# A transformer kernel with streamed weights: low parts written over the raw steps, experts written out, the first norm moved into the first modulation

## The reference, cut to what matters

```python
def first_block(x, c, w_ada, ...):                    # two layers
    cs = jax.nn.silu(c)
    for l in range(DEPTH):
        mod = cs @ w_ada[l] + b_ada[l]
        shift, scale, gate = mod[:, None, :D], mod[:, None, D:2 * D], mod[:, None, 2 * D:]
        h = rmsnorm(x, g_pre[l]) * (1.0 + scale) + shift
        y = hybrid_mixer(h, ...)                      # block attention, compressed and windowed attention
        x = x + gate * rmsnorm(y, g_post[l])
    return x
def second_block(x, c, w_ada, ...):
    # layer 0: neighbourhood attention, then a gated feed-forward of width 2816
    # layer 1: latent attention, then 8 experts of width 1792, the best 2 per token
    ...
        x = x + g_a[:, None, :] * m
        h = _modulate(x, sh_f, sc_f)
        ...
        x = x + g_f[:, None, :] * f
    return _rmsnorm(x) * final_norm
```

## Time and profile before

| what | us |
|---|---|
| median of 3 runs (lowest, highest) | 1647.71 (1645.18, 1649.2) |
| profiled execution | 1648.49 |
| its span | 1646.7 |
| mean granted clock of PE | 0.94 |
| PE busy | 1420.0 |
| DVE busy | 1216.3 |
| ACT busy | 861.3 |
| POOL busy | 65.5 |

### The profile page before, as it was taken

One profiled execution on the slowest core, in us unless ns is written; L12 is line 12 of the kernel. 1 busy time (PEld: TensorE's weight loads), 2 busy tenths in 40 slices (PEclk: granted clock), 3 DMA queues, 4 the chain that ended last, 5 costly groups with the idle time before them and its releaser, 6 DMA issues.

```text
span 1646.7 us, 21231 instructions
## 1 busy us (share of the span) xinstructions
PE 1420.0 (86%) x7628; PEld 1189.7 (72%) x7628; DVE 1216.3 (74%) x1484; ACT 861.3 (52%) x1210; POOL 65.5 (4%) x82
## 2 busy tenths in 40 slices
PE   2798996989869986899985896999999999999992
PEld 1687776877658865898974785877777777777772
DVE  8676657766566646788866535889889888899885
ACT  0443544435443543344323544577677777777772
POOL 0000000000010000000001004000000000000001
PEclk9989998999988997999997996999999999999996
DMA  9763524735246632677773214799999999999782
GB/s 400 296 258 110 198 103 162 283 118 193 102 155 254 238 120 97 258 309 282 267 270 122 103 52 145 272 342 364 353 343 366 341 351 366 336 368 353 289 366 89
DMA packets 61538, 403.08 MB, mean 245 GB/s; under 512 B 6535, under 2 KB 9735, under 8 KB 15117
## 3 DMA queue, kind: packets, MB, share of 16 engines
q1 hardware_dynamic: 52416, 379.45, 60.7%
q10 hardware_dynamic: 7020, 15.17, 2.6%
q0 software_dynamic: 2016, 7.34, 1.2%
HBM read 393.01 MB, written 8.91 MB: 244 GB/s over the span
## 4 chain that ended last, share of the span: by engine, by line
PE 49%; DVE 31%; ACT 9%; issue 7%; DMA 2%; POOL 1%; ACTq 0%; DVEq 0%; SPq 0%; POOLq 0%
DVE w_lo L2175 18%; PE PS L826 13%; PE PS L828 12%; PE PS L827 12%; ACT w_hi L1601 4%; DVE acc L2192 3%; ACT xg L1695 2%; PE PS L978 1%; PE PS L998 1%; DMA raw<-in_ws 1%; DVE a_lo L2335 1%; PE PS L896 1%; DVE hb L2346 1%; DVE hb L2344 1%; DVE h_lo L2301 1%
## 5 line engine op out<-in xcount | busy, mean ns | idle before, releaser
L2175 DVE TENSOR_TENSOR w_lo<-raw,w_hi 128x2048 fp32r<-128x2048 f32 x287 | 659.5, 2298 | 147.7 <-ACT w_hi L1601 124.8
L1601 ACT ACTIVATE w_hi<-raw 128x2048 fp32r<-128x2048 f32 x287 | 547.7, 1918 | 235.1 <-PE PS L828 222.9
L826 PE MATMUL PS<-w_hi,h_hi 128*128 128x512 f32 (+2 forms) x812 | 336.6, 415 | 24.7 <-DVE h_lo L2596 7.3
L827 PE MATMUL PS<-w_lo,h_hi 128*128 128x512 f32 (+2 forms) x812 | 319.4, 393 | 0.0
L828 PE MATMUL PS<-w_hi,h_lo 128*128 128x512 f32 (+2 forms) x812 | 319.2, 393 | 0.0
L826 PE MATMUL PS<-h_hi,w_hi 128*128 128x256 f32 x776 | 235.4, 303 | 24.1 <-DVE h_lo L2220 11.2
L828 PE MATMUL PS<-h_hi,w_lo 128*128 128x256 f32 x776 | 227.1, 293 | 0.0
L827 PE MATMUL PS<-h_lo,w_hi 128*128 128x256 f32 x776 | 227.1, 293 | 0.0
L826 PEld LDWEIGHTS PS<-w_hi,h_hi 128*128 128x128 f32 x812 | 156.3, 192 | 72.0 <-DVE w_lo L2175 15.1
L2192 DVE SCALAR_TENSOR_TENSOR acc<-raw,cs,acc 128x512 f32<-128x512 f32 x252 | 189.5, 752 | 8.9
L828 PEld LDWEIGHTS PS<-w_hi,h_lo 128*128 128x128 f32 x812 | 156.1, 192 | 32.7
(11 more groups left out here) (310 smaller groups left out, 1405.8 us busy)
## 6 DMA issues: line engine op xcount, KB each, us to landing
raw<-in_ws SPq DMA_DIRECT2D x359, 1024.0 KB, 5.7
y_rows<-ysb ACTq DMA_DIRECT2D x10, 512.0 KB, 7.0
rp<-in_rp ACTq DMA_DIRECT2D x8, 384.0 KB, 4.7
ckb<-in_ck ACTq DMA_DIRECT2D x2, 1024.0 KB, 4.8
y_rows<-ones ACTq DMA_DIRECT2D x3, 512.0 KB, 9.2
x<-in_x SPq DMA_DIRECT2D x1, 1024.0 KB, 11.3
gpost<-in_gpost ACTq DMA_DIRECT2D x2, 512.0 KB, 5.3
x_rows<-xn_f ACTq DMA_DIRECT2D x2, 512.0 KB, 3.8
```

The lines of the kernel that those rows point to most:

```text
L826: t.matmul(out, lhs[0], rhs[0], start=start, stop=False, skip_group_check=True)
L827: t.matmul(out, lhs[0], rhs[1], start=False, stop=False, skip_group_check=True)
L1601: a.activation(wh[:, SPL_AT[e.phase][i], :], raw[:, r, :], ACT.Copy).then_inc(*e.inc("hi"))
L2175: v.tensor_tensor(wl[:, s, :], raw[:, r, :], wh[:, s, :].bitcast(F32), ALU.subtract).then_inc(*e.inc("raw_used"))
```

## The change

1. The rings: RAW is 8 instead of 6, SPL 4 instead of 3, and w_lo has no ring of its own: it is written over the raw step it is made of (twelve places of 8 KB per partition as before). A weight step's raw place is therefore released by PE's `split_used`, a half's as before by `raw_used`. `hi_to` and `split_to` go one step further in most places.
2. The experts are written out, moe0 to moe7, on every engine; only `more` is a loop.
3. pre holds units 0 to 3 (8 halves). x is fetched behind its fourth step, lc behind its eighth. ACT's squares and DVE's xn of the first norm stand inside pre, PE's turn behind unit 1. ACT makes the w_hi of four steps before the scaled half of h; DVE makes w_lo(0) behind h_lo. The gate units 4 and 5 of the first layer are summed behind w2 to w5 of lay0 and added on PE between its first slots; the gate's product with gpost stands in tick 1.
4. Halves stand elsewhere: in the layers behind w7 to w15 (nothing behind w2 to w5 in lay1), in na as formerly in the layers (none behind w6). PE adds units 0 and 1 in ticks 1 and 4 instead of before tick 0.

```diff
-RAW = 6
-SPL = 3
+RAW = 8
+SPL = 4
-LAY_ADA = {9: 2, 10: 3, 12: 4, 15: 5}
+LAY_ADA = {1: 0, 4: 1, 9: 2, 10: 3, 12: 4, 15: 5}
...
-def layer_steps():
-    halves = dict(zip((2, 3, 4, 5, 7, 8, 9, 10, 11, 12, 13, 14), (x for j in range(6) for x in ada_steps(j))))
+def layer_steps(gates):
+
+    place = [(6, 0, 0), (7, 0, 1), (8, 1, 0), (8, 1, 1), (9, 2, 0), (10, 2, 1), (10, 3, 0), (11, 3, 1),
+             (12, 4, 0), (13, 4, 1), (13, 5, 0), (14, 5, 1)]
     out = []
     for n in range(20):
         out.append(("w", n))
-        if n in halves:
-            out.append(halves[n])
+        if gates and n in (2, 3, 4, 5):
+            out.append(("ada", 4 + (n - 2) // 2, n % 2))
+        out += [("ada", j + 6 * gates, half) for after, j, half in place if after == n - 1]
     return out
...
-    halves = dict(zip(range(2, 14), (x for j in range(6) for x in ada_steps(j))))
+    halves = dict(zip((2, 3, 4, 5, 7, 8, 9, 10, 11, 12, 13, 14), (x for j in range(6) for x in ada_steps(j))))
...
+def raw_released(p, i):
+
+    if STEPS[p][i][0] == "w":
+        return "split_used", STEPS[p][i][1]
+    return "raw_used", i
+
+
+RAW_AT, RAW_NEED = ring_plan(RAW, {p: len(STEPS[p]) for p in PHASES}, raw_released)
+SPL_AT, SPL_NEED = ring_plan(SPL, SPLITS, lambda p, i: ("split_used", i))
...
-        wl = sb("w_lo", [P, SPL, STEP], F32R)
+
+        wl = nc.alloc_sbuf_tensor_at("w_lo", [P, RAW, STEP], F32R, offset=at[0] - 4 * RAW * STEP - 4 * SPL * STEP)
...
-                        sp.wait_ge(*e.at("raw_used", RAW_NEED[phase][i]))
+                        sp.wait_ge(*e.at(*RAW_NEED[phase][i]))
...
+                    if phase == "pre" and i == 3:
+                        sp.dma_start(x[:], dram["x"]).then_inc(*e.inc("x_in", 16))
+                    if phase == "pre" and i == len(STEPS[phase]) - 1:
+                        sp.dma_start(lc[:], dram["lc"]).then_inc(*e.inc("lc_in", 16))
...
+                    if i in (2, 5):
+                        pe.wait_ge(*e.at("bank3", used[3]))
...
+                    if i == 1:
+                        pe.wait_ge(*e.at("cmp_u", 1))
+                    if i == 4:
+                        pe.wait_ge(*e.at("clogits", 1))
                     if i in LAY_ADA:
-                        ada(LAY_ADA[i])
+                        ada(unit + LAY_ADA[i])
...
-                with dve.Fori(0, LOOPS) as rep:
-                    for p in TWO:
-                        start(p, rep)
-                        expert()
-                start("moeZ")
-                expert()
+                for p in EXPERTS[1:]:
+                    start(p)
+                    expert()
...
-                        v.tensor_tensor(wl[:, s, :], raw[:, r, :], wh[:, s, :].bitcast(F32),
+                        v.tensor_tensor(wl[:, r, :], raw[:, r, :], wh[:, s, :].bitcast(F32),
                                         ALU.subtract).then_inc(*e.inc("raw_used"))
...
+            raw_to(4)
+            e.enter("lay0")
+            normed(xn_l)
+            e.resume("pre")
             raw_to(99)
...
-                    split_to(min(na_steps_before(i) + SPL, 15) if i < 14 else 16)
+                    split_to(min(na_steps_before(i) + SPL, 16))
```

More of the change, by code:

```diff
@@ L31 @@
 T_CMP = 15
-PHASES = ["pre", "lay0", "lay1", "na", "ffn", "mla", "rt", "go", "moe0", "moeA", "moeB", "moeZ", "more", "end"]
+EXPERTS = [f"moe{i}" for i in range(NEXP)]
+PHASES = ["pre", "lay0", "lay1", "na", "ffn", "mla", "rt", "go"] + EXPERTS + ["more", "end"]
 MORE = 2 * S // (P + 1)
 ROUNDS = NEXP + MORE
-TWO = ("moeA", "moeB")
-LOOPS = (NEXP - 2) // 2
-REPS = {"moeA": LOOPS, "moeB": LOOPS, "more": MORE}
-EXPERTS = [("moe0", 0)] + [(p, r) for r in range(LOOPS) for p in TWO] + [("moeZ", 0)]
-KIND = {"lay0": "lay", "lay1": "lay"}
+REPS = {"more": MORE}
+KIND = {"lay0": "lay", "lay1": "lay", **{p: "moe" for p in EXPERTS}}
 LAY_FEAT = (0, 1, 4, 5)
@@ L129 @@
 STEPS = {
-    "pre": [x for j in range(6) for x in ada_steps(j)],
-    "lay0": layer_steps(),
-    "lay1": layer_steps(),
+    "pre": [x for j in range(4) for x in ada_steps(j)],
+    "lay0": layer_steps(True),
+    "lay1": layer_steps(False),
     "na": na_steps(),
@@ new lines, in ring_plan @@
+        for _ in range(reps):
+            here = dict(totals)
+            for i in range(n):
+                last = owner[place[p][i]]
+                if last is not None:
+                    k = (last[0], last[1] + 1 - here.get(last[0], 0))
+                    assert need[p][i] is None or need[p][i][0] == k[0]
+                    need[p][i] = k if need[p][i] is None else max(need[p][i], k)
+                name, j = released(p, i)
+                owner[place[p][i]] = (name, here.get(name, 0) + j)
+            for name, n_ in (("raw_used", len(STEPS[p])), ("split_used", SPLITS[p])):
+                totals[name] = totals.get(name, 0) + n_
@@ L204 @@
+    "act_lo": {"moe": 7, "more": 7},
+    "act_tok": {"moe": 7, "more": 7},
+    "act_turned": {"moe": 7, "more": 7},
+    "ada_sum": {"pre": 4, "lay0": 8, "lay1": 6, "na": 6, "ffn": 12},
     "bank0": {"lay": 5, "na": 3, "ffn": 8, "mla": 3},
@@ L206 @@
     "bank2": {"lay": 4, "na": 3, "ffn": 7, "mla": 3},
-    "bank3": {"pre": 6, "lay": 6, "na": 6, "ffn": 12, "mla": 3},
+    "bank3": {"pre": 4, "lay0": 8, "lay1": 6, "na": 6, "ffn": 12, "mla": 3},
     "bank4": {"mla": 1},
@@ L238 @@
     "downs_done": {"end": 1},
-    "dve": {"pre": 38, "lay": 82, "na": 47, "ffn": 105, "mla": 31, "rt": 10, "go": 23, "moe0": 11, "moeA": 7, "moeB": 7, "moeZ": 7, "more": 7},
+    "dve": {"pre": 26, "lay0": 93, "lay1": 81, "na": 46, "ffn": 104, "mla": 29, "rt": 10, "go": 23, "moe0": 11, "moe1": 7, "moe2": 7, "moe3": 7, "moe4": 7, "moe5": 7, "moe6": 7, "moe7": 7, "more": 7},
     "dve_end": {"end": 21},
@@ L249 @@
     "hb_act": {"lay": 4, "na": 4, "ffn": 4, "mla": 4},
-    "hi": {"lay": 20, "na": 16, "ffn": 33, "mla": 9, "moe0": 21, "moeA": 21, "moeB": 21, "moeZ": 21, "more": 21},
+    "hi": {"lay": 20, "na": 16, "ffn": 33, "mla": 9, "moe": 21, "more": 21},
     "k_sum": {"mla": 2},
@@ L292 @@
     "sel": {"go": 2},
[L293 removed]
+    "split_used": {"pre": 4, "lay": 20, "na": 16, "ffn": 33, "mla": 9, "moe": 21, "more": 21},
     "sq": {"lay": 4, "na": 2, "ffn": 2, "mla": 6, "rt": 2, "end": 2},
     "stored": {"end": 2},
[L296 removed]
+    "tanh": {"ffn": 22, "moe": 7, "more": 7},
     "token_of": {"go": 2},
```

260 lines of the change are left out of this document (125 added, 135 removed), and 8 rows, old and new, of the table COUNTS.

## The result

The changed kernel takes **1661.4 us** (median of four runs, 1660.3 to 1662.4) against 1647.7: a ratio of 1.0079, 95% interval [1.0064, 1.0095]. It is slower, by 13.7 us between the medians and by 10.5 to 15.7 us by the interval. Forecast was 1638, and the time lies outside the range of 1625 to 1654. The profiled execution took 1661.0 us, its span 1659.2.

The account below looks back on a forecast made before the run. PE was taken as the bound everywhere but in pre. The terms 7.2 - 4.0 + 7.2 - 7.4 + 2.0 + 0 - 0.6 + 6.0 = +10.4 us, off the profiled 1648.5, gave 1638 us; range 1625 to 1654.

Parts of the forecast that it names:

- Head, +7.2: Start up to the first product of a weight: it begins at 53.5 instead of 60.75, gaining 7.2 us.
- The gate units' -4.0: lay0: two gate units moved there from pre, at 2.07 us each on PE, cost 4.0 us.
- Ticks, -7.4: Tick 8 of both layers: w12 waits for w9's place, so PE waits for exp, 3.7 us in each layer.
- Ticks, +7.2 for the stalls that vanish: Both layers: PE's stalls of 3.59 and 3.60 us for modc go, as unit 4's first half moves a tick later.
- The wait for clogits: Layers' ticks: the forecast is wrong if PE reaches its new wait for clogits before DVE has done them; no size given.
- The +2.0 at lay1's start: lay1's start: waits of 1.00 and 0.99 us go, since units 0 and 1 moved into ticks 1 and 4.
- The other reuses have a place released by a half's sum, or one whose step was finished over half a tick earlier: Layers' ticks: reuses of raw places other than w12's were given no price.
- na 0, ffn -0.6, mla 0: na: +3.3 for a vanished wait against -3.3 for three landings; ffn: -0.6 for the first slot; mla: 0.
- Experts, +6.0: Six loop experts written out gain 1.0 us each, 6.0 in all; ends 0 and 8.4.
- A: Rival, lay0, lay1 and na: held places stall PE at four more reuses, 3.7 us each, giving 1653 us; chance 0.20.
- B: Rival: experts don't gain, through the fourth w_lo ahead of act_lo or the stream; 1644 us, 1647 with less head gain; chance 0.20.
- A's condition: Rival A decides if ACT's and DVE's lead on PE at that tick is under 9 us (landing, w_hi and w_lo).

Follow-up runs that it names:

- e1: The kernel before with only the eight experts written out, rings, start and places as they were: 1639.27 us, 0.9938 of before.
- e2: Changed kernel with rings undone (raw 6, w_hi 3, w_lo its own 3, place free once w_lo is made), na's halves back: 1635.13 us, 0.9901 of before.
- e3_w12free: Changed kernel with one half moved ahead of w9 in both layers, so w12 takes a half's place instead of w9's: 1658.96 us, 1.0051 of before.
- e9: Changed kernel with ACT's and DVE's lead in the experts alone set to three steps instead of four: 1651.64 us, 1.0023 of before.

## Why the prediction was wrong

Forecast was -10.4 us, and the traces differ by +12.4. Of the 22.8 between them 15.2 lie in the layers (steps 2 to 4 below), 6.3 in experts 1 to 6 and 6.2 in the last (step 6); na, ffn to router, moe0 and the head together came out 4.9 better.

**1. Head, +7.2: right.** The first product starts at 53.83, forecast 53.5. The gate units' -4.0 wasn't measured alone: from e1 to e2, lay0 grows by 1.4 us, PE's busy time in it by 1.8 and its waits hardly change. That points to some 2 us for two units, so my term was on the high side.

**2. Ticks, -7.4: the step that failed by size.** The new wait is the one named, at the place named and by the landing named (4.8 against 4.9 taken), and the exps of the chain end at 158.4, near the 159.2 forecast. But the wait measures 6.25 and 6.29, not 3.7. I dated PE's need from the turn of tick 8 (155.48). After the change PE stops at 153.36, at the tick's first piece, behind

```profile
152.71 0.65 PE L981 MATMUL PS<-kswz,qn 128*128 128x256 f32 x2
```

since ACT's qm copy (L1817, 158.74) frees that piece's bank, and this copy stands behind the exps and a ptp in ACT's order. With tick 7's turn 0.6 earlier than before (147.72 against 148.28), the turn of tick 8 was due at 154.9. PE stopped 1.5 us ahead of it and was let go 1.3 us after the exps: 3.7 + 1.5 + 1.3 = 6.5 against the 6.25 measured.

**3. Ticks, +7.2 for the stalls that vanish: failed.** They vanished, but not as a gain. Without any held place (e2) PE waits 2.92 in tick 8 for two halves ahead of one w_lo, and 3.02 in tick 4 for clogits. In e1, which has the old order, it waits 3.60 for modc and 2.98 for y. The stall of the old order came back as one of nearly the same size two ticks earlier. I had read which half left tick 8 and not what the tick before it received. The wait for clogits is one of the signs of being wrong that the prediction named (3.00 and 3.53 in the changed kernel). The +2.0 at lay1's start didn't come either: the 1.00 and 0.99 are the 2.01 at 314.27 (2.00 in e2). With +7.2 - 4.0 + 2.0 I forecast +5.2 for the layers without the held places; e2 gives -3.1 against before.

**4. "The other reuses have a place released by a half's sum, or one whose step was finished over half a tick earlier": failed.** This sentence priced the rest of the held places at nothing. e3_w12free sets w12 free, and the wait turns up as 7.04 and 4.88 elsewhere. Set against e2, the held places and the deeper rings cost 7.8 us in lay0 and 6.5 in lay1, 14.3 for the 7.4 forecast. The larger wait in tick 8 holds 3.3 of it in each layer, the wait for the gate in lay0's first tick (3.67 at 94.30, none in e2) as much again; in lay1 1.9 of the rest is PE's busy time (183.5 against 181.7), and the remainder is spread over several waits. How much of the 14.3 is the held places' and how much the depth's, no run divides. The whole of the layers: 8.3 short by step 3, 6.9 by steps 2 and 4, together the 15.2 between -2.2 forecast and -17.4 measured.

**5. na 0, ffn -0.6, mla 0: right in the numbers, na's reasons in part.** ffn, mla and router came out 0.4 better. In na new waits took the place of the 3.31: 2.10 at 530.03 (0.70 before), 1.66 at 548.74 and 0.82 at 556.24, of about the size that the prediction gave its three (4.8 less 3.5 is 1.3 each, not 1.1). But only the first stands behind a landing, as forecast; ahead of the other two ACT has no such row, and DVE is busy with halves and w_lo.

```profile
530.03 1.96 PE L1265 MATMUL PS<-nakz,naq 128*128 128x512 f32 x4 [2.10 <-ACT nakz L1971]
525.67 1.91 ACT L1617 ACTIVATE w_hi<-raw 128x2048 fp32r<-128x2048 f32 x1 [3.32 <-DMA raw<-in_ws]
```

So PE's idle time in na grew by 1.2 us, and its busy time fell by 4.0 (144.9 at a granted clock of 0.94, before 148.9 at 0.90). Busy time in na differs by 3 us between executions of like kernels (below), so the 2.8 us by which na came out better aren't evidence for the change.

**6. Experts, +6.0: the second failure.** The direct price of the loop form was read rightly as 1.4 (e1: 8.4 us in all). But the depth took it back. I did write that "depth 4 puts one w_lo more ahead of the first act_lo", and allowed 0.4 us for it: a w_lo is 2.30 us, and act_lo is on PE's path. It cost 1.0 in each of the first four, 2.6 and 2.4 in the next two (where the clock fell as well), and 2.6 of the last one's 6.2. e9 takes 9.8 us of the median back by one step of depth. The other 3.6 of the last expert stay in e9, with the wait of 4.33 before the padded extra round; the prediction has no term for it. That a ring of 4 doesn't divide 21, as three does, stood in the code.

**7. The rivals.** What came about is A and B together: held places win in the layers, by A's mechanism (landing, w_hi, w_lo and the exps behind PE's release), with the deeper lead as a partner whose share is open; and the experts don't gain, for the first of B's two reasons. I gave them 0.20 each as alternatives, though nothing excludes the one with the other: both together, 1653 + 6 = 1659, is within 3 us of what was measured, though by step 3 partly by luck. A range up to 1654 treated them as exclusive. A's condition, a lead of ACT and DVE on PE under 9 us, was in the text with the reading "6 to 7 us", and so the condition was met on my own numbers; I went by how long before a step had been used instead.

## What to carry to other kernels

When a ring's places come to be freed by a later engine, count places anew, with the whole chain behind a release (landing and both passes, here 9 us) against the producers' lead on the consumer: in the two layers six places with depth 3 lost 12.7 us here, eight with depth 4 lost 14.3, nine with depth 3 nothing. What share of the 14.3 is the deeper lead's is open. Deeper prefetch isn't free either, where the prefetch shares a program order with what the consumer waits for: one w_lo more of 2.3 us ahead of a_lo cost 1.0 us in each of the first four written-out experts after moe0 and more in the next two, so put the consumer's next need first, then the prefetch. Date the need of the consumer by the first of its instructions that anything behind the stalled one releases, not by the one at which the data is used.
